# Moving the sine layers of the Hyena filter into the second MLP's upward GEMM, and joining three stages of latent attention, on one Trainium2 core

## The reference, cut to what matters

```python
x = x + (relu(rmsnorm(x) @ mlp_w1[1]) ** 2) @ mlp_w2[1]     # 512 x 1024, hidden 4096
x = rmsnorm(x, norm_final)
# Hyena filter, depends on constants and weights only; positions 0..511 and 0..255
h = sin(freq * (z @ w1 + b1)); h = sin(freq * (h @ w2 + b2)); h = sin(freq * (h @ w3 + b3))  # 64 wide
h = (h @ w4) * decay                                        # 1024 wide: forward and backward taps
spectrum = rfft(two_sided(h) / sum(abs(h)))                 # as matrix products with cosine and sine tables
# latent attention: a = (adaptive norm of x or ctx) @ w_in, 256 query, 128 key/value, 32 rotary columns
q = rmsnorm(rms_norm(a_q) @ w_uq);  ckv = rms_norm(a_kv);  k_nope, v = split(ckv @ w_ukv)
```

## Time and profile before

| | us |
|---|---|
| median of 3 runs | 3555.27 (3551.01 to 3558.55) |
| time of the profiled execution | 3550.53 |
| its span, first to last instruction | 3548.8 |
| PE busy | 3235.8 (91%) |
| DVE, ACT, POOL busy | 1634.5, 1019.3, 1089.9 |

### The profile page before, as it was taken

One profiled execution on the slowest core, in us unless ns is written; L12 is line 12 of the kernel. 1 busy time (PEld: TensorE's weight loads), 2 busy tenths in 40 slices (PEclk: granted clock), 3 DMA queues, 4 the chain that ended last, 5 costly groups with the idle time before them and its releaser, 6 DMA issues. The chain is left out here.

```text
span 3548.8 us, 55536 instructions
## 1 busy us (share of the span) xinstructions
PE 3235.8 (91%) x21694; PEld 2523.9 (71%) x21694; DVE 1634.5 (46%) x2411; ACT 1019.3 (29%) x1530; POOL 1089.9 (31%) x518
## 2 busy tenths in 40 slices
PE   7987878999999789998898899999999689899999
PEld 6855767787877568786386378888888333389987
DVE  6833543421131632213675347555555355557741
ACT  4322232222222531222120023222233224433322
POOL 3422112444433035443031012222232005534433
PEclk9978999999999899999899999999999879999999
DMA  3224344222223022223011111111111011022222
GB/s 132 95 97 166 111 134 143 90 100 89 95 92 99 1 77 95 89 95 133 31 60 61 59 42 56 63 65 59 55 64 59 28 46 44 19 84 95 89 88 84
DMA packets 78395, 282.16 MB, mean 80 GB/s; under 512 B 9306, under 2 KB 12192, under 8 KB 77229
## 3 DMA queue, kind: packets, MB, share of 16 engines
q1 hardware_dynamic: 77676, 279.52, 23.5%
q10 hardware_dynamic: 576, 0.62, 0.1%
HBM read 270.12 MB, written 2.12 MB: 77 GB/s over the span
## 5 line engine op out<-in xcount | busy, mean ns | idle before, releaser
L207 POOL TENSOR_TENSOR weights_low<-weight_ring,weights_high 128x1024 fp32r<-128x1024 f32 x359 | 890.7, 2481 | 1845.8 <-ACT weights_high L201 1845.8
L201 ACT ACTIVATE weights_high<-weight_ring 128x1024 fp32r<-128x1024 f32 x372 | 392.3, 1055 | 853.0 <-PE bank L260 842.4
L258 PE MATMUL bank<-ffn_in_high,weights_low 128*128 128x258 f32 (+2 forms) x1408 | 438.5, 311 | 10.1 <-DVE ffn_in_low L459 6.3
L260 PE MATMUL bank<-ffn_in_high,weights_high 128*128 128x258 f32 (+2 forms) x1408 | 437.8, 311 | 0.0
L259 PE MATMUL bank<-ffn_in_low,weights_high 128*128 128x258 f32 (+2 forms) x1408 | 437.5, 311 | 0.0
L258 PEld LDWEIGHTS bank<-ffn_in_high,weights_low 128*128 128x128 f32 x1408 | 266.8, 189 | 26.2 <-issue 6.8
L259 PEld LDWEIGHTS bank<-ffn_in_low,weights_high 128*128 128x128 f32 x1408 | 267.4, 190 | 14.7
L260 PEld LDWEIGHTS bank<-ffn_in_high,weights_high 128*128 128x128 f32 x1408 | 266.2, 189 | 14.2
L258 PE MATMUL bank<-mlp_down_high,weights_low 128*128 128x512 f32 x512 | 201.1, 393 | 8.4 <-DVE mlp_down_low L559 8.4
L258 PE MATMUL bank<-mlp_in_high,weights_low 128*128 128x512 f32 x512 | 201.5, 394 | 7.3 <-DVE mlp_in_low L459 6.2
L259 PE MATMUL bank<-mlp_down_low,weights_high 128*128 128x512 f32 x512 | 201.1, 393 | 0.0
(11 more groups left out here) (538 smaller groups left out, 6443.3 us busy)
## 6 DMA issues: line engine op xcount, KB each, us to landing
weight_ring<-in_mod SPq DMA_DIRECT2D x96, 512.0 KB, 4.5
weight_ring<-in_ffn_up SPq DMA_DIRECT2D x88, 512.0 KB, 3.4
weight_ring<-in_mlp_up SPq DMA_DIRECT2D x64, 512.0 KB, 3.4
weight_ring<-in_mlp_down SPq DMA_DIRECT2D x64, 512.0 KB, 3.5
weight_ring<-in_ffn_down SPq DMA_DIRECT2D x44, 512.0 KB, 3.5
weight_ring<-in_gdn_in SPq DMA_DIRECT2D x32, 512.0 KB, 3.5
weight_ring<-in_dswa_in SPq DMA_DIRECT2D x27, 512.0 KB, 3.5
weight_ring<-in_fh_in SPq DMA_DIRECT2D x16, 512.0 KB, 3.5
```

Of the source, the lines that this page charges most:

```text
L201: act.activation(self.high[:, (g.s0 + at) % SPLIT, 0:g.floats], raw, ACT.Copy).then_inc(self.high_ready, 1)
L207: pool.tensor_tensor(self.low[:, slot, 0:g.floats], self.ring[:, (g.c0 + at) % RING, 0:g.floats], self.high[:, slot, 0:g.floats], ALU.subt ...
L258: pe.matmul(bank, wl, ah, start=start, stop=False)
L260: return pe.matmul(bank, wh, ah, start=False, stop=stop)
```

## The change

1. **Sines in the MLP.** A new class `FilterSines` holds the three layers. The second MLP's upward stage takes it as `among`: behind tiles 4, 12 and 20 (`cuts`) PE does a layer's two products, DVE its reduction, ACT its sine. SP loads z, w1 and w23 at the head of that stage. The sines wait in the memory of ctx.
2. **Filter stage.** It begins with the taps. w4 is loaded first, decay in six pieces with a semaphore for each, then the tables; ctx when all taps are multiplied. `norm.sums` stands behind the last mix on DVE, `norm.tensor` behind the fourth spectrum group on PE, `norm.roots` behind the absolute values on ACT, `norm.scale` behind the sixth scaled group. The spectrum's banks are 7, 0, 1, 2 in place of 6, 7, 0, 1.
3. **One stage `mla_heads`.** Norms, values, queries and keys are one stage. Values no longer wait for the normalized latent: PE multiplies the latent times its gain, and ACT scales by the inverse root for each token while it copies out. For that PE sums squares into 12 columns by token as well (2 moving columns a product). rope and constants load from the head of the stage.

```diff
+class FilterSines:
+    cuts = (4, 12, 20)
+    def load(self, sp):
+        for dst, src in ((self.z, "filter_z"), (self.w1, "filter_w1"), (self.w23, "filter_w23")):
+            sp.dma_start(whole(dst), self.a[src]).then_inc(self.loaded, 16)
+    def tensor(self, pe, layer):
+        if layer:
+            pe.wait_ge(self.sines, layer)
...
+        for bank, (lo, hi) in zip(self.banks, self.HALVES):
+            last = pe.matmul(bank[0:self.W, 0:hi - lo], weights, src[:, lo:hi], start=True, stop=True)
+        last.then_inc(self.sums, 1)
+    def vector(self, dve, layer):
...
+        dve.wait_ge(self.sums, layer + 1)
...   (the same 8 instructions as L2106 to L2113)
+        dve.tensor_scalar(u[:, :], u[:, :], self.PI, -self.PI, ALU.min, ALU.max).then_inc(self.reduced, 1)
+    def scalar(self, act, layer):
+        act.wait_ge(self.reduced, layer + 1)
+        act.activation(self.sn[:, :], self.u[:, :], ACT.Sin).then_inc(self.sines, 1)
...
     def split_high_all(self, act, g, norm, among=None):
         done = self.split_high_first(act, g, norm)
+        lo = done
+        for step, cut in enumerate(among.cuts if among else ()):
+            rounds(act, lo, cut + done, RING, lambda n, at, turn: self.split_high(act, g, n, at, turn))
+            among.scalar(act, step)
+            lo = cut + done
...
     def multiply_tiles(self, pe, g, streams, drained, norm, beside=None, among=None):
...
+        for step, cut in enumerate(among.cuts if among else ()):
+            rounds(pe, lo, cut, RING, tile)
+            among.tensor(pe, step)
+            lo = cut
...   (mlp_stages: DVE's loop over tiles is cut in the same way)
 def hyena_filter_stage(core, a, sn, Hr, Hi, cs, norm, loads):
+                sp.dma_start(w4[:, :], a["filter_w4"]).then_inc(w4_loaded, 16)
+                for b in range(BLOCKS):
+                    sp.dma_start(decay[:, :, b, :], a["filter_decay"][:, :, b, :]).then_inc(decay_loaded[b], 16)
                 cs.load(sp, loaded)
+                sp.wait_ge(tap_sums, 2 * BLOCKS)
                 load_beside(sp, loads, loads_done)
...
+                pe.wait_ge(w4_loaded, 16)
...
-                pe.wait_ge(norm.rooted, 1)
+                pe.wait_ge(loaded, 16 * cs.loads)
...
+                            if n == nb:
+                                norm.tensor(pe)
...
-                            if n == nb:
+                            if n == 2 * nb - 2 and s == 0:
                                 norm.scale(dve, norm_order)
...
+def mla_heads_stage(core, a, g_v, g, at, qa, ckv, v, qn, qr, kn, kr):
             def _(pe):
+                pe.wait_ge(kv_squared, 1)
+                for b in range(BLOCKS):
+                    last = pe.matmul(ps[7][:, 2 * b:2 * b + 2], sq[:, 2, b * P:(b + 1) * P], core.ones[:, 0:2], start=True, stop=True)
...   (sums of the kv squares over 512 and 256 tokens, then of the query squares, two products of 512)
+                pe.wait_ge(kv_weighed, 1)
+                for n in range(2 * BLOCKS):
+                    if n >= 4:
+                        pe.wait_ge(values_kept, n - 3)
...   (12 value products), then the three products of L2648 to L2650
+                pe.wait_ge(values_kept, 2 * BLOCKS)
+                pe.wait_ge(kv_ready, 1)
                 for p in range(8):
...
+                act.activation(sq[:, 2, :], at[:, 2, :], ACT.Square).then_inc(kv_squared, 1)
...
+                dve.tensor_scalar(weighed[:, :], at[:, 2, :], core.params("kv_a"), None, ALU.mult).then_inc(kv_weighed, 1)
...   (ACT: roots by token, of kv, of q; then 12 scaled copies. DVE: reciprocals and products as in L2539 to L2544)
```

More of the change, by code:

```diff
@@ L611, in _ @@
                 def _(pe):
-                    core.multiply_tiles(pe, up, [(parts, core.ps[0:RING])], drained, norm)
+                    core.multiply_tiles(pe, up, [(parts, core.ps[0:RING])], drained, norm, among=among)
                 @block.vector
@@ L626, in tile @@
                                           relu[:, at % 2, :], ALU.mult)
-                    rounds(dve, 0, up.tiles, up.per, tile)
+                    lo = 0
+                    for step, cut in enumerate(among.cuts if among else ()):
+                        rounds(dve, lo, cut, up.per, tile)
+                        among.vector(dve, step)
+                        lo = cut
+                    rounds(dve, lo, up.tiles, up.per, tile)
         residual_gemm_stage(core, name + "_down", down, [(tiles_of(hid), core.x, T, None)])
@@ L2004, in zero_edges @@
     return dve.memset(padded[:, :, JOINT + 1:JOINT + 2], 0.0)
-def hyena_filter_stage(core, a, Hr, Hi, cs, norm, loads):
-    W = 64
-    EMB = 33
+class FilterSines:
+    SIGNALS = ("mlp_loaded", "mlp_sums", "reduced", "sines", "angle_order")
+    W, EMB = 64, 33
+    cuts = (4, 12, 20)
     TWO_PI = 2.0 * math.pi
@@ new lines, in signals @@
+    def signals(self, sems):
+        self.loaded, self.sums, self.reduced, self.sines, self.order = sems
+    def load(self, sp):
[4 more added lines that the diff above has]
+            pe.wait_ge(self.sines, layer)
+        else:
+            pe.wait_ge(self.loaded, 16 * 3)
+        weights, src = (self.w23[:, layer - 1, :], self.sn) if layer else (self.w1[:, :], self.z)
+        for bank, (lo, hi) in zip(self.banks, self.HALVES):
+            last = pe.matmul(bank[0:self.W, 0:hi - lo], weights, src[:, lo:hi], start=True, stop=True)
+        last.then_inc(self.sums, 1)
@@ L2097, in _ @@
                 norm_order = Order(dve, norm.order)
[L2098 to L2114, removed]
                 def mix(b):
@@ L2127, in _ @@
                 mix(BLOCKS - 1)
+                norm.sums(dve, norm_order)
                 n = 0
@@ L2142, in _ @@
                 norm.squares(act)
[L2143 to L2147, removed]
                 for b in range(BLOCKS):
@@ L2154, in _ @@
                         act.activation(ab[:, d, :], f[:, d, b, :], ACT.Abs).then_inc(absed, 1)
+                norm.roots(act)
 class Tables:
@@ L2510, in _ @@
                     dve.tensor_scalar(dst, dst, shift[:, n, s:s + 1], None, ALU.add)
[L2513 to L2545, removed]
```

149 lines of the change are left out of this document (97 added, 52 removed).

## The result

| | us |
|---|---|
| median after, 4 runs | 3509.76 (3500.02 to 3512.14) |
| median before, 4 runs | 3553.40 (3551.01 to 3558.55) |
| ratio | 0.9873, 95% interval 0.9861 to 0.9884 |
| profiled execution after, and its span | 3512.14, 3510.1 |

The kernel became 43.6 us faster; forecast were 45.7, from 3555.3 (three runs of the kernel before) to 3509.6. A second set of four runs gave 3516.38 (3506.32 to 3517.67), ratio 0.9897 (0.9883 to 0.9911), against 3553.68.

What follows compares the result with a forecast made beforehand. PE was taken to bound the MLP's upward stage, while it idled in the filter stage's head and latent attention's three short stages. +4.3 - 30.0 + 3.0 - 23.0 = -45.7 took 3555.3 to 3509.6 us; range 3497 to 3527.

Steps and rivals of the forecast that it cites:

- Sines in the MLP, +4.3: Second MLP's upward stage: PE pays the three layers' products in full, +4.3 us (3.9 to 7.7); DVE and ACT work covered.
- the 1.3 us a layer that I counted: Upward stage: weight cut and POOL's low half take 4.1 of a tile's 5.4 us, leaving 1.3 us a layer free.
- Taps begin 30.0 us earlier: Filter stage: without sines, the first product waits only for w4, taken as 2.9 us (2.3 to 3.8); gain 30.0 us.
- Taps take as long as before: Filter stage: taps keep their 28.13 us, starting at half clock as before; -3 us if the clock rises sooner.
- Tail +3.0: Filter stage's end: the late norm.scale puts the second reciprocal on the path, +3.0 us (1 to 6).
- the forecast for the filter stage, -27.0: Whole filter stage: taps 30.0 us earlier, tail 3.0 us longer, -27.0 us in all.
- Latent attention -23.0: Joined latent attention stage: key projections 22.0 us earlier and 1.0 more from full clock, -23.0 us (-18 to -27).
- the -1.0 of the forecast: Latent attention: key projections find a full clock where the old ones began at half, saving 1.0 us more.
- DMA as the bound of the filter stage: Rival, 5%: filter stage's loads run at half rate and hold the spectrum by up to 23 us; 3533 us.
- Values at half clock: Rival, 2%: latent attention's sums and values all run at half clock, -11 us in place of -23; 3522 us.
- Tables loaded again in each cut: Rival, 2%: ACT reloads both tables in each cut of 28 tiles, +1.2 us a tile, 35 us; 3544 us.
- Sines that stall the GEMM: Rival, 9%: ACT's wait for the reduction holds the weight cut; 2 to 7 us a layer, 3515 to 3530 us.

Runs made afterwards that it cites:

- the longer reduction: Kernel after with six more vector instructions in each sine layer's reduction, values unchanged: 3518.69 us, ratio 0.9908 to the kernel before.
- The early w4: Kernel after with w4 loaded in the second MLP's upward stage, so the first tap product waits for nothing: 3507.85 us, ratio 0.9874 to the kernel before.
- The second profile: Profiled execution from a rerun of the kernel after, unchanged; that set of runs measured 3516.38 us, ratio 0.9897 to the kernel before.
- the sines alone: Kernel after with latent attention in its three old stages: 3537.04 us, ratio 0.9963 to the kernel before; rerun 3536.52 us, 0.995.

## Why the prediction was right

**Sines in the MLP, +4.3: +4.5.** In the nine profiles with the sines as they are the up stage is 187.7 to 187.8 us, in the three without 183.2. The layers' products cost what they were priced at, and nothing else reached PE. The reduction, the sine and its table load were covered: ACT waited 0.3 us at most for DVE, POOL's low half never held PE, and there was one table load of 1.28 us, not three. The Trainium skill (ScalarE: Activation LUTs, "Table sets: the hidden batching unit") says that copies are in every set; here the trace agrees, with no load on the copy at 1346.92; the 26 loads of the earlier trace rows ahead of such copies are all there in the kernel after too, and why stayed open. The cover was larger than the 1.3 us a layer that I counted: the longer reduction puts it at 4.3. I had left ACT's idle time between sine and cut, 2.30 us in the kernel after, out of that count; it makes 3.6 of the 4.3.

**Taps begin 30.0 us earlier: 29.3.** w4 came at 3.7 us, not 2.9, near the upper bound of 3.8. The Trainium skill (DMA: Bandwidth & Descriptors, "Anatomy of one DMA — SWDGE (gpsimd) path") gives the 2.0 us + bytes/436e3 behind the forecast's 2.6 us as a fit to DMAs that GpSimd issues. This one SP issues, so the forecast carried the rule over to another path, and there the trace's 3.7 us doesn't bear it out. The early w4 shows that this error costs little: decay comes only at 4.4.

**Taps take as long as before: right in most executions.** This term was taken as equal, with the half clock of the old taps read as 9 us; the trace has 11.2, two of them inside the 0.95 of the next row. In the profiled execution it was +4.1, since the clock stayed at half for 19.6 us. Of the other seven profiles whose taps wait for w4 as here, one took 32.1 us, one 28.6, and five 27.3 to 27.7, up to 0.9 less than before. It is the term with the widest spread, and the largest part of the difference between the forecast for the filter stage, -27.0, and the -22.4 of the profiled execution; with an early rise the stage gave -27.4.

**Tail +3.0: +2.8.** Both halves of the working held: the reciprocal behind `norm.scale` (1.9) and the norm's sum on PE (0.9).

**Latent attention -23.0: -21.9.** Key projections begin 23.6 us earlier, not 22.0: all 24 value instructions ran at full clock (10.46 us, where I took 11.3), and the sums were a little shorter. From there to the query projections it took 18.8 us in place of 19.9, the -1.0 of the forecast. What I didn't have was given back behind them: from the query projections to the end of the stage it is 74.1 us against 71.4. Two stretches, before and after:

```profile
2826.41:2897.83 71.42, 61.90 (x164) 24.07 (x160) 41.40 (x51) 13.49 (x24) 0.00 (x0) 0.84 0.09 30
2784.96:2859.06 74.10, 64.51 (x164) 25.00 (x160) 41.57 (x51) 13.49 (x24) 0.00 (x0) 0.81 0.09 29
```

The same 164 instructions are there, and the same waits of PE for DVE (4.2, 2.6 and 1.2 us). What differs is the granted clock, 0.84 against 0.81, and PE's busy time, 2.6 us longer: more of the stretch fell at half clock. The eight other profiles with this joined stage unchanged show the same 74.1 to 74.3 us, so it belongs to the change and not to one execution.

**The rivals.** DMA as the bound of the filter stage: DVE waited for PE's first product and not for decay, and no product of the spectrum waited for a load. Values at half clock: they ran at 1.00. Tables loaded again in each cut: one load in the stage. Sines that stall the GEMM: not here, but 8 us more of reduction make it so.

**The sum.** In the profiled execution 0.5 (ahead of the second MLP) + 4.5 - 1.3 (down stage, whose code is unchanged; the granted clock is 0.98 before and 0.99 after) - 22.4 + 1.8 (to latent attention) - 21.9 = -38.8, and the span is 38.6 shorter. The four runs of that set lie between 3500.02 and 3512.14, and the forecast started from a median 1.9 us above that of the result's four runs of the kernel before, while its gain was 2.1 too large. So the agreement of median and forecast to 0.2 us is luck. The second profile, with the early rise, has a span of 3504.3, 44.5 below. Over all eight runs the gain is 41, so the forecast was some 4 us too good. Of the stretches that the change touches, the taps have the widest spread: the clock can rise late in them (+4), and I had bounded that term only from the other side (-3). How much of the 4 us it makes isn't shown, since the untouched stretch ahead of the second MLP spreads by 14 us between profiles.

## What to carry to other kernels

Small work of idle engines can be moved into a stretch that PE bounds at the price of its PE instructions alone, but price the cover in the queue that feeds PE (here ACT's cut and POOL's low half) and test it by lengthening the moved work. When the first of several loads is brought forward, the next load is what the stage waits for. After a stage that leaves PE idle, count its next 20 us of matmuls at either clock. Profile more than once before a few microseconds are put down to the code, and compare stage by stage: here the stages' lengths repeat within 0.4 us where the clock does the same, while whole executions of one kernel differ by 12 us and more.

## What the runs showed of the hardware

The clock's rise is not a fixed time behind the start of work. With PE busy throughout, the same taps ran at the level of 1.2 GHz for 9.4 to 11.2 us in eight profiles, for 12.1 in one and for 19.4 and 19.6 in two; the kernel after and the sines alone, each profiled twice, have one of either kind. In the two profiles with w4 loaded in the MLP it was 13.0 and 13.3 us: the taps began sooner, and the clock rose as far into the stage as before, 13.0 and 13.3 us. In the kernel after the clock fell at about the filter stage's start; with eight more products in the gap it fell 5.4 us into the stage, with the taps already running.

A table load that stands ahead of a waiting ACTIVATE is issued before the wait: in the longer reduction it ran 8 us before its sine (1337.62 and 1345.81). It cost nothing there.
